# Gate and up of the FFN by Strassen over both halves of K, sums carried in PSUM, two weight sums by DMA

## The reference

```python
def rms_norm(x, g):
    xf = x.astype(jnp.float32)
    y = xf * lax.rsqrt(jnp.mean(xf * xf, axis=-1, keepdims=True) + EPS)
    return (y * g.astype(jnp.float32)).astype(x.dtype)

def swiglu(h, w_gate, w_up, w_down):
    return (jax.nn.silu(h @ w_gate) * (h @ w_up)) @ w_down
...
        x = x + rms_norm(m.astype(x.dtype), norm_mix_post[layer])
        h = rms_norm(x, norm_ffn_pre[layer])
        f = swiglu(h, ffn_w_gate[layer], ffn_w_up[layer], ffn_w_down[layer])
        x = x + rms_norm(f.astype(x.dtype), norm_ffn_post[layer])
```

## Time and profile before

| | us |
|---|---|
| median of 3 runs | 2219.3 |
| lowest, highest | 2217.36, 2220.44 |
| span of the profiled execution | 2217.0 |
| PE busy | 2199.2 |
| DVE busy | 1692.9 |
| ACT busy | 1173.1 |
| POOL busy | 304.2 |
| DMA | 416.52 MB, 188 GB/s mean |

### The profile page before, as it was taken

The page is one execution under the profiler, slowest core; times in us unless marked ns, Lnnn a source line. Parts: engine busy times, 40 slices in busy tenths (PEclk is TensorE's granted clock), DMA queues, the critical chain, the costliest instruction groups (busy, mean ns, idle before and its releaser), DMA issues.

```text
span 2217.0 us, 26301 instructions
## 1 busy us (share of the span) xinstructions
PE 2199.2 (99%) x10011; PEld 1810.1 (82%) x10011; DVE 1692.9 (76%) x1686; ACT 1173.1 (53%) x1330; POOL 304.2 (14%) x247
## 2 busy tenths in 40 slices
PE   8999999999999999999999999999999999999998
PEld 7888888888888888888887787788888888888886
DVE  5587467988888888888755655778888898888886
ACT  6677544654454454444655555546555454544543
POOL 0851000300000000000021001004000000000001
PEclk9999999999999999999999999999999999999999
DMA  9555446456656555564564445455656545566552
GB/s 309 186 169 169 166 133 209 152 191 228 227 190 208 191 172 186 192 228 175 167 209 152 152 152 166 169 190 179 228 190 218 198 169 175 189 228 227 190 190 95
DMA packets 213883, 416.52 MB, mean 188 GB/s; under 512 B 12328, under 2 KB 14976, under 8 KB 213248
## 3 DMA queue, kind: packets, MB, share of 16 engines
q1 hardware_dynamic: 213040, 414.29, 54.8%
q10 hardware_dynamic: 720, 0.56, 0.1%
HBM read 412.73 MB, written 2.10 MB: 187 GB/s over the span
## 4 chain that ended last, share of the span: by engine, by line
PE 97%; DVE 1%; DMA 1%; issue 0%; ACT 0%; SPq 0%; POOLq 0%; POOL 0%; DVEq 0%; ACTq 0%
PE acc L1263 73%; PE acc L1276 12%; PE tp L1292 2%; PE sc L1276 2%; PE pv L1276 2%; PE sc L1374 1%; DMA raw<-in_ev_w_in 1%; PE pv L1403 1%; PE sc L1370 1%; PE pv L1398 1%; PE sc L1353 0%; PE pv L1353 0%; DVE w_lo L1527 0%; SPq L789 0%; PE pv L1292 0%
## 5 line engine op out<-in xcount | busy, mean ns | idle before, releaser
L1527 DVE TENSOR_TENSOR w_lo<-raw,w_hi 128x2048 fp32r<-128x2048 f32 x301 | 689.5, 2304 | 57.7 <-PE acc L1263 40.8
L931 ACT ACTIVATE w_hi<-raw 128x2048 fp32r<-128x2048 f32 x301 | 572.9, 1911 | 152.4 <-PE acc L1263 105.9
L1263 PE MATMUL acc<-w_hi,h_hi 128*128 128x512 f32 x1576 | 432.6, 396 | 3.8 <-ACT h_hi L903 3.8
L1263 PE MATMUL acc<-w_lo,h_hi 128*128 128x512 f32 x1576 | 423.1, 390 | 0.0
L1263 PE MATMUL acc<-w_hi,h_lo 128*128 128x512 f32 x1576 | 422.1, 390 | 0.0
L1263 PEld LDWEIGHTS acc<-w_lo,h_hi 128*128 128x128 f32 x1576 | 296.0, 188 | 62.7
L1263 PEld LDWEIGHTS acc<-w_hi,h_lo 128*128 128x128 f32 x1576 | 295.6, 188 | 61.9
L1263 PEld LDWEIGHTS acc<-w_hi,h_hi 128*128 128x128 f32 x1576 | 291.2, 188 | 63.4 <-issue 6.9
L931 ACT ACTIVATE w_hi<-gx 128x2048 fp32r<-128x2048 f32 x70 | 134.4, 1920 | 221.0 <-DVE gx L1540 83.8
L931 ACT ACTIVATE w_hi<-queries 128x2048 fp32r<-128x2048 f32 x70 | 134.4, 1920 | 220.4 <-DVE queries L1540 83.9
L1263 PE MATMUL acc<-w_hi,y_hi 128*128 128x512 f32 x832 | 224.6, 392 | 0.7 <-ACT y_hi L1135 0.7
(11 more groups left out here) (240 smaller groups left out, 2321.8 us busy)
## 6 DMA issues: line engine op xcount, KB each, us to landing
raw<-in_ffn_w_gate SPq DMA_DIRECT2D x68, 1024.0 KB, 5.8
raw<-in_ffn_w_up SPq DMA_DIRECT2D x68, 1024.0 KB, 5.2
raw<-in_ffn_w_down SPq DMA_DIRECT2D x48, 1024.0 KB, 7.7
raw<-in_od_w_in SPq DMA_DIRECT2D x48, 1024.0 KB, 5.1
raw<-in_ev_w_in SPq DMA_DIRECT2D x37, 1024.0 KB, 5.4
queries<-in_ffn_w_down SPq DMA_DIRECT2D x20, 1024.0 KB, 6.9
gx<-in_ffn_w_down SPq DMA_DIRECT2D x20, 1024.0 KB, 7.0
raw<-in_ev_w_out SPq DMA_DIRECT2D x16, 1024.0 KB, 5.1
```

The lines of the kernel that those rows point to most:

```text
L931: act.activation(w_hi[u % HI][:, :, :], raw[place.buf][:, :, :], ACT.Copy).then_inc(hi_done, 1)
L1263: mm = pe.matmul(acc[n % 2][t][:, :], operand(lhs, a, k, t), w[:, k, :], start=first and k == 0 and j == 0, stop=last and k == KT - 1 and ...
L1527: dve.tensor_tensor(w_lo[u % LO][:, :, :], raw[plan.place[u].buf][:, :, :], w_hi[u % HI][:, :, :].bitcast(F32), ALU.subtract).then_inc(lo_ ...
```

## The change

- **Strassen over both halves of K.** Quarters 2 and 3 go through seven products too (pair B beside pair A). A body has P1 to P7 for A and B, 14 single products, and d0 to d3 of two each: 22 products of 12 matmuls. It has 18 units instead of 15. The same products of A and B follow each other into the same PSUM bank.
- **Sums carried in PSUM.** P6, P7, P2, P4 and P3 no longer start a bank: P1's bank (`corner`, the bank `sc`) is copied to another bank by ACT, and both go on accumulating; likewise P5's bank (`upper`, `pv`). Four ACT copies a body, two DVE additions (`upper_part`), none on POOL. The signs are turned so that weight sums are additions; the gating uses the negative of the norm factor (`nrstd`).
- **Down accumulates in PSUM.** ACT copies `yacc` into one of three banks (`seed`), the matmuls add to it, ACT copies it back (`unload`): eight of each in a body, in place of DVE's eight additions.
- **Weight sums.** Six are formed by DVE, and two (P7A, P7B: `u1` onto `u0` and `u3` onto `u2`) by a DMA that adds, issued by POOL (`transfer`).
- **Six buffers.** `gq`, which holds the gain vector at the boundaries, is the sixth `raw` buffer in bodies; the gains are loaded later. The second key tile `kz` moves into memory that the bodies reuse, and is cleared again in layer 1.
- **Order.** The down products come early in a body, the last unit of a body is P4B, and the transposes of the gated rows stand behind P1A of the next body. P1 of the first body is no longer in the head.
- **Left sums.** `left_sums` makes eight instead of four, with eight more POOL instructions in each layer.

```diff
-BLOCK_RAW = 5
+BLOCK_RAW = 6
+POST_GAIN = 5
...
-ENTRIES = ("P1", "P5", "P3", "P6", "g2", "P2", "P7", "P4", "u3", "g3", "u2", "d0", "d1", "d2", "d3")
-LOADS = ("u1", "u0", "g0", "g2", "g1", "u3", "g3", "u2", "d0", "d1", "d3", "d2")
-EARLY = ("g0", "u0")
-FORMS = ("P5", "P6", "P7", "P4")
+ENTRIES = ("P1A", "P1B", "d0", "d1", "P5A", "P5B", "P6A", "P6B", "P3A",
+           "P3B", "P7B", "P7A", "d2", "P2A", "P2B", "d3", "P4A", "P4B")
+DOWNS = ("d0", "d1", "d2", "d3")
+LOADS = ("g0", "g2", "u0", "d0", "u2", "d1", "u1", "u3", "d2", "g1", "d3", "g3")
+EARLY = LOADS[:3]
+FORMS = ("P5A", "P5B", "P6A", "P6B", "P4A", "P4B")
+TRANSFERS = ("P7A", "P7B")
+PAIRS = {"A": (0, 1), "B": (2, 3)}
+BANKS = 3
...
+        if name[0] == "g":
+            return (read("P2" + pair), added("P4" + pair)) if second else (read("P4" + pair),)
+        return (read("P3" + pair), added("P6" + pair), added("P7" + pair)) if second else (read("P7" + pair),)
...
-        lefts = sb("lefts", [P, 2, 2, KT, P], F32R)
+        lefts = [sb(f"lefts{i}", [P, 2, 2, KT, P], F32R) for i in range(2)]
...
+            def copy(body, name):
+
+                act.wait_ge(unit_done, body.last(name) + 1)
+                src, dst = {"P1": (corner, gate_low), "P6": (corner, spare[1]), "P7": (corner, spare[2]), "P5": (upper, spare[3])}[name]
...
+                act.activation(dst, src, ACT.Copy).then_inc(copied[name], 1)
+
+            def seed(body, j, t):
...
+                    act.activation(down_banks[k], yacc[:, t, j * KC:(j + 1) * KC], ACT.Copy).then_inc(seeded, 1)
+
+            def unload(body, j, t):
...
+                act.activation(yacc[:, t, j * KC:(j + 1) * KC], down_banks[k], ACT.Copy).then_inc(drained[k], 1)
...
+            def upper_part(body, t):
+
+                if t == 0:
+                    dve.wait_ge(unit_done, body.last("P3") + 1)
+                    dve.wait_ge(copied["P6"], body.index + 1)
+                    dve.tensor_tensor(spare[1], upper, spare[1], ALU.add).then_inc(up_done[0], 1)
+                else:
+                    dve.wait_ge(copied["P5"], body.index + 1)
+                    dve.wait_ge(copied["P7"], body.index + 1)
+                    dve.tensor_tensor(spare[3], spare[2], spare[3], ALU.add).then_inc(up_done[1], 1)
...
                 pool.wait_ge(pv_done, plan.heads_of[layer])
...
+                sums("A", spare, len(LEFT) * layer)
+                pool.wait_ge(upd_done, 1 + max(plan.update[b, c, t] for c in range(NC) for t in range(NT)))
+                sums("B", later, len(LEFT) * layer + 4)
+
+            def transfer(body, name):
+
+                total, part = plan.place[body.index, weight_of(name)], plan.place[body.index, addend_of(name)]
+                pair = name[2]
+                if name[:2] == "P7":
+                    pool.wait_ge(landed[total.buf], 16 * total.count)
...
+                        pool.wait_ge(form_done, body.form["P5" + pair])
...
+                pool.wait_ge(landed[part.buf], 16 * part.count)
+                pool.dma_start(raw[total.buf][:, :, :], raw[part.buf][:, :, :], accum_op=ALU.add).then_inc(transferred[name], 16)
```

More of the change, by code:

```diff
@@ new lines, in block @@
+                high(body, "P5B")
+                copy(body, "P1")
+                unload(body, 0, 0)
+                seed(body, 1, 1)
+                unload(body, 0, 1)
+                seed(body, 2, 0)
+                high(body, "P6A")
+                unload(body, 1, 0)
+                seed(body, 2, 1)
+                unload(body, 1, 1)
+                seed(body, 3, 0)
+                if body.first:
+                    left_high("S3B", body.layer)
+                    left_high("S2B", body.layer)
@@ new lines, in block @@
+                high(body, "P6B")
+                high(body, "P3A")
+                copy(body, "P5")
+                if body.first:
+                    left_high("S4B", body.layer)
+                high(body, "P3B")
+                high(body, "P7B")
+                high(body, "P7A")
+                copy(body, "P6")
+                high(body, "d2")
+                high(body, "P2A")
+                copy(body, "P7")
+                high(body, "P2B")
+                unload(body, 2, 0)
+                high(body, "d3")
@@ new lines, in block @@
+                unload(body, 2, 1)
+                seed(body, 3, 1)
+                high(body, "P4A")
+                if body.next:
+                    seed(body.next, 0, 0)
+                high(body, "P4B")
+                silu_part(body, 0)
+                high_next("P1A")
+                unload(body, 3, 0)
+                if body.next:
+                    seed(body.next, 0, 1)
+                unload(body, 3, 1)
+                high_next("P1B")
+                if body.next:
+                    seed(body.next, 1, 0)
@@ L1215, in _ @@
                     block(body)
-                block_hi(part.tail)
+                silu_part(part.bodies[-1], 1)
+                for t in range(NT):
+                    block_high(part.tail, t)
         @block.tensor
@@ new lines, in block @@
+                low(body, "d0")
+                form(body, "P5B")
+                block_low(body, 0)
+                block_low(body, 1)
+                low(body, "d1")
+                low(body, "P5A")
+                form(body, "P6A")
+                if body.first:
+                    left_low("S1B", body.layer)
+                low(body, "P5B")
+                form(body, "P6B")
+                low(body, "P6A")
+                if body.first:
+                    left_low("S3B", body.layer)
+                    left_low("S2B", body.layer)
@@ new lines, in block @@
+                low(body, "P6B")
+                low(body, "P3A")
+                if body.first:
+                    left_low("S4B", body.layer)
+                low(body, "P3B")
+                low(body, "P7B")
+                low(body, "P7A")
+                low(body, "d2")
+                upper_part(body, 0)
+                form(body, "P4A")
+                low(body, "P2A")
+                upper_part(body, 1)
+                form(body, "P4B")
+                low(body, "P2B")
+                low(body, "d3")
@@ L1887, in _ @@
+                low(body, "P4A")
+                low(body, "P4B")
+                gated(body, 0)
+                low_next("P1A")
+                if body.next:
+                    form(body.next, "P5A")
+                low_next("P1B")
             for section in plan.parts:
@@ L1893, in _ @@
                     block(body)
-                block_lo(section.tail)
+                gated(section.bodies[-1], 1)
+                for t in range(NT):
+                    block_low(section.tail, t)
         @block.gpsimd
@@ L2037, in _ @@
                 for body in section.bodies or ():
-                    spreads(body)
+                    transfer(body, "P7A")
+                    transfer(body, "P7B")
 def log_counts():
```

569 lines of the change are left out of this document (293 added, 276 removed).

## The result

The changed kernel takes 2290.3 us (2285.7 to 2294.8, four runs) against 2218.9 for the one before: ratio 1.032, interval 1.031 to 1.034, so **3.2% slower**, where 2195.3, 1.1% faster, was predicted; the range ended at 2250. The profiled run's span is 2283.9 us, 66.9 more than before and 90.9 more than the forecast span of 2193.0.

The account below looks back on a forecast made before the run. PE alone was taken to bound the 20 bodies: 2217.0 - 54.4 (matmuls) + 3.6 (`lefts`) + 24 (head) + 2.8 (tail) = 2193.0 us span; as median of runs 2195.3, 1.1% faster. Range 2172 to 2250.

Parts of the forecast that it names:

- The matmuls and `lefts`: PE in the 20 bodies: 12 fewer matmuls each, -54.4 us; 24 more at the slower `lefts` pace, +3.6 us.
- The order walk: One body walked in order across PE, DVE, ACT and loads: low P2B ready at 47.5, wanted at 47.9, stall 0.
- The transfers' price: Each DMA that adds in a body: a load plus one more pass of 2.7 us, 7.8 us.
- Rival 1: Transfers in the bodies become the bound: 13.2 us each, 152 us more, 2347; decides from 9.4 us on; chance 0.17.
- the limit of 28.8: Two transfers in a body: done at 25.6 us, limit 28.8; each us past it is a us of every body.
- Rival 2: The bodies' 0.4 us margin is gone through late loads or busy ACT: 1 to 2 us a body, 2225; chance 0.12.
- The head: Before each layer's bodies: pair B's sums delay the root; PE idles 8.8 + 0.4 us, slow clock 1.5: +24 us.
- the forecast's own range: From the head (8 to 46 us) and `lefts`: 2172 to 2215, with chance 0.57 for the forecast.
- u0's early load: At the boundaries: the gain vector loads later into the sixth buffer, with units of 5.4 us ahead of its reader: 0.
- The tail: End of each layer's bodies: P4B last, nothing covers SiLU and gating; net 1.4 us a layer, +2.8.
- DVE's lag behind the head: After the head of each layer's bodies: DVE starts about 1.5 us behind.

Follow-up runs that it names:

- buf_yhi: buf with ACT making the down operand's high parts ahead of those of d1 and P5A, P1 left in its bank: 2245.6 us.
- buf_noadd: buf with the two adding transfers and their waits left out, so the output lacks those terms: 2242.4 us.
- buf: The changed kernel with d2 loaded into u1's buffer instead of u3's, so it is issued earlier: 2256.7 us.
- bank_yhi: buf plus bank, with ACT making the down operand's high parts ahead of those of d1 and P5A: 2223.2 us.
- early: The changed kernel with the third early load (u0) issued behind the loads of the head's fourth to sixth units: 2270.2 us.
- root: The changed kernel with POOL taking the reciprocal root ahead of pair B's eight sums: 2282.6 us.
- no_root: bank_yhi plus early, and in a layer's last body SiLU, operand parts and gating ahead of the next unit's parts on ACT and DVE: 2197.1 us.
- bank: The changed kernel with P1 computed in the bank of gate's upper rows and ACT's copy going the other way: 2286.3 us.

## Why the prediction was wrong, point by point

**The matmuls and `lefts`: right.** -54.4 + 3.6 gave a body of 60.95 us; where nothing waits it takes 61.13. The saving is real, and in the change waits bury it. `lefts` still runs slower (0.93 us per four against 0.907); why is open.

**The order walk: the step that failed.** "Margin 0.4 us, stall 0" came out as 3.5 us a body (64.4 less 60.95), 62 us over the 18 intervals. Three things were missing in it.
- *The operand on ACT.* I let DVE make the operand's low parts at once after the transposes. Its high part stood on ACT behind d1's, which waits for a load. DVE lost 1.5 us, u3 was issued 1.1 late. buf_yhi shows what the order was worth: 11.1 us.
- *u3 beside the transfer.* I gave it 8 us; it took 8.9 to 11.4 in 15 of 18 bodies, where it was issued behind the transfer, as the walk itself had it (9.4 against 9.1). The walk had no row for what two transfers in flight do to each other by their order. buf_noadd prices it at 14.3 us on buf; it is largely the same loss as the one before, seen from its other end.
- *P1A behind the SiLU.* P1A opens the bank in which P4B ended. I had written that between bodies P1A covers the SiLU, and overlooked that both use one bank: 1.1 us a body, 22.4 us by bank_yhi against buf_yhi (19.5 by body intervals).

The buffer that d2 takes ties these together: the planner counted u1 as free only at P7A's place in the order, behind u3, so d2 took u3's buffer and waited for low P3B. The walk used that order and did not ask what it cost: 33.6 us by buf, some 4 of them at the tail.

**The transfers' price: right in size, wrong as a limit.** 7.8 forecast, 8.1 measured (7.0 to 11.3). The Trainium skill (*DMA: Bandwidth & Descriptors*, Anatomy of one DMA, with the rule of *Collectives: The Full Stack*, The bandwidth ceiling) gave an estimate of 6.8, below every one of them. Rival 1 said that past 9.4 us each us is a us of every body, and put the two transfers one behind the other. They overlap: in bank_yhi both take longer at the median, 10.4 us, and the second is still in before the limit of 28.8. What would happen with the second past 28.8 us in every body no run shows.

**Rival 2 (margin gone)** named the mechanism, at 1 to 2 us a body; it was 3.5, so its 2225 and its chance of 0.12 were both too low. I had the margin at 0.4 us of 60.95 and still gave the forecast 0.57. A walk with a margin under the spread of its own landing times (5.1 to 5.7, 7.8 behind others) should have been the less likely case.

**The head: right in place, and in size partly by luck.** 8.8 + 0.4 forecast, 8.9 idle and the slow clock behind it measured. But five of pair B's eight sums ran beside DVE, not two and a half, which made them 5.7 us longer than forecast; the stall that u0 caused held PE back by 11 us and pair A's sums by 5, and hid it. In early, without that stall, the idle is 10.2 us a layer. That the root behind pair B causes it: root (17.9 to 3.2). Of the 24 us forecast 14.5 come back by moving it where the bodies have slack, 7.8 where they have none. One sum is off by 2 us: 2195.3 + 22 is 2217, where the forecast's own range was written to end at 2215; nothing else rests on it.

**u0's early load, costed at 0: wrong.** "The gain vector loads later into the sixth buffer" looked at the gain vector's reader only. It is u0 that must wait for the gain vector's last use, ahead of three loads of the head on SP's in-order queue: 20.1 us by early. This was the second failed step.

**The tail: +2.8 forecast, 11.2 us of idle and about 4 of slow clock (1.4 and 2.5, from the starts of the matmuls behind it against 0.91 us per four).** I had left out ACT's row: two high parts for the next units, the second of them waiting for its load, stood ahead of the SiLU. no_root shows the forecast's size (1.2 us a layer) with that order mended.

Together: 62 for the bodies, 23 for u0 and the clock behind it, 12 for the tail (15 less the 2.8 forecast): 97, less 3 us for DVE's lag behind the head, which did not show: 94, for the 90.9 that were missing. The 3 us between them are not explained.

## What to carry to other kernels

When work is taken from the engine that bounds, walk every other engine's row in order, with each wait for a load and what is queued behind it, and treat a margin smaller than the spread of the landing times as a stall. Ask for each moved or added load what stands behind it in the queue of its issuer, not only who reads it, and for two transfers that will be in flight together which is issued first. And undo suspected parts together as well as alone: bank gave 4 us alone and 22 where the next late thing had been removed.

## What was not expected of the hardware

A 1 MB transfer that adds, SBUF to SBUF, landed in 7.0 to 12.5 us. What the 1 MB load beside it took went by which of the two was issued first: in the change the load took 6.2 to 7.3 us when it was issued with the transfer or just ahead of it, and the transfer 11.2 to 11.3; when it came 0.25 us or more behind, the load took 8.9 to 11.4 and the transfer 8.1 to 11.2. Without the transfer the load took 5.0 to 5.4 (buf_noadd, layer 0). Steady bodies agree within 0.02 us (61.12 to 61.14) once PE never waits, while waiting ones vary by 5 us (61.4 to 66.1).
